# Expert sums kept in two arrays of half the columns, each block's add done as two adds

## The reference

```python
top_i, top_w = route(h2, p["w_router"], p["router_bias"])      # 8 of 64 experts per token
ffn = (routed_experts(h2, top_i, top_w, w_exp_gate, w_exp_up, w_exp_down)
       + swiglu(h2, w_sh_gate, w_sh_up, w_sh_down))              # one shared expert
x = x + g2 * ffn
# routed_experts: rows sorted by expert, each expert's rows in blocks of 128
out = lax.map(block, (row_tok, blk_exp))                         # swiglu of a block with its expert's weights
out = out.reshape(n_rows, D) * row_w[:, None]
return jax.ops.segment_sum(out, row_tok, num_segments=T + 1)[:T] # sum over a token's 8 rows
```

## Time and profile before

| | |
|---|---|
| median of three runs | 2139.46 us |
| the profiled execution | 2142.09 us, its span 2140.1 us |
| PE busy | 1930.8 us, 90% of the span |
| DVE, ACT, POOL busy | 1044.5, 871.8, 407.8 us |
| granted TensorE clock, mean | 0.955; 1.00 in every stretch of the expert stage up to 2050 us |
| expert stage | some 1104 to 2088 us of the span |
| one issue on SP, median | 0.32 us for `acc_d<-ysh`, 0.46 us for `aa<-acc_d` (9 each) |

### The profile page before, as it was taken

How to read it: one execution, slowest core, us unless ns; L and a number is a source line. 1 busy time by engine, 2 the same in 40 slices (tenths; PEclk the granted TensorE clock), 3 DMA queues, 4 the chain that set the end, 5 groups by cost and what they waited for, 6 DMA issues and landing times. The chain is left out here.

```text
span 2140.1 us, 33737 instructions
## 1 busy us (share of the span) xinstructions
PE 1930.8 (90%) x10175; PEld 1508.7 (70%) x10177; DVE 1044.5 (49%) x1519; ACT 871.8 (41%) x1181; POOL 407.8 (19%) x337
## 2 busy tenths in 40 slices
PE   3799999899899997988789999999899999999960
PEld 3799999899788565865447777666566776776740
DVE  3312401255337333555426666565555666666646
ACT  4210111333203212221246666666565666666642
POOL 0100000211111000000112333232333323223320
PEclk9899999999899998999889999999999999999985
DMA  6211221111253665325069999999999899879946
GB/s 239 71 49 49 97 70 30 34 56 50 80 190 119 222 220 197 118 100 199 0 239 386 294 298 296 368 311 374 374 330 352 281 286 287 265 236 307 283 91 257
DMA packets 154835, 433.66 MB, mean 203 GB/s; under 512 B 11551, under 2 KB 76307, under 8 KB 130210
## 3 DMA queue, kind: packets, MB, share of 16 engines
q1 hardware_dynamic: 120338, 307.40, 38.2%
q0 software_dynamic: 31776, 116.05, 21.0%
q10 hardware_dynamic: 2672, 9.57, 1.1%
HBM read 351.27 MB, written 81.72 MB: 202 GB/s over the span
## 5 line engine op out<-in xcount | busy, mean ns | idle before, releaser
L1999 DVE TENSOR_TENSOR wexp_lo<-wexp,wexp_hi 128x2048 fp32r<-128x2048 f32 x190 | 427.1, 2289 | 50.2 <-ACT wexp_hi L1951 46.7
L1951 ACT ACTIVATE wexp_hi<-wexp 128x2048 fp32r x190 | 353.0, 1905 | 55.5 <-issue 54.3
L1932 PE MATMUL bank<-wexp_down,hTe 128*128 x736 | 331.0, 592 | 1.9 <-ACT hTe L1969 1.9
L1907 PE MATMUL bank<-wexp_hi,x_hi 128*128 128x512 f32 x744 | 300.0, 403 | 3.8 <-DVE wexp_lo L1999 3.8
L1907 PE MATMUL bank<-wexp_hi,x_lo 128*128 128x512 f32 x744 | 291.6, 392 | 0.0
L1907 PE MATMUL bank<-wexp_lo,x_hi 128*128 128x512 f32 x744 | 290.1, 390 | 0.0
L1881 POOL DMA_INDIRECT acc_d<-ob,ixs x92 | 154.0, 1673 | 607.3 <-DMA acc_d<-ob,ixs 339.4
L1932 PEld LDWEIGHTS bank<-wexp_down,hTe 128*128 128x128 f32 x736 | 138.9, 189 | 142.5 <-issue 135.6
L491 PE MATMUL bank<-hT_hi,w_hi 128*128 128x344 f32 x576 | 187.2, 325 | 3.0 <-DVE w_lo L575 3.0
L491 PE MATMUL bank<-hT_hi,w_lo 128*128 128x344 f32 x576 | 185.1, 321 | 0.0
L491 PE MATMUL bank<-hT_lo,w_hi 128*128 128x344 f32 x576 | 184.5, 320 | 0.0
(11 more groups left out here) (327 smaller groups left out, 2919.3 us busy)
## 6 DMA issues: line engine op xcount, KB each, us to landing
wexp<-in_w_exp_gate SPq DMA_DIRECT2D x64, 1024.0 KB, 9.2
wexp<-in_w_exp_up SPq DMA_DIRECT2D x64, 1024.0 KB, 12.6
wexp_down<-in_w_exp_down SPq DMA_DIRECT2D x64, 1024.0 KB
wada<-in_w_ada SPq DMA_DIRECT2D x12, 2048.0 KB, 11.2
w_raw<-in_w_in SPq DMA_DIRECT2D x44, 512.0 KB, 3.9
gates_d<-gst POOLq DMA_DIRECT2D x48, 172.0 KB, 2.1
gate<-gates_d SPq DMA_DIRECT2D x16, 516.0 KB, 5.4
xn<-in_x_prompt ACTq DMA_DIRECT2D x8, 512.0 KB
```

Of the source, the lines that this page charges most:

```text
L1907: last = pe.matmul(banks[0][:].rearrange("p (g n) -> p g n", g=2), stat[:, b, k, :], mov[:, b, :, k * FF:(k + 1) * FF], start=(k == 0 and ...
L1932: last = pe.matmul(banks[4 + half][:], hT[:, f, :], wdn[:, bass.ds(slot, 1), f, half * 512:half * 512 + 512].rearrange("p a n -> p (a n)") ...
L1951: act.activation(w_hi[:, b, g, :], wexp[:, bass.ds(e & (RING - 1), 1), g, :].rearrange("p a n -> p (a n)"), ACT.Copy).then_inc(whi_ok, 1)
L1999: dve.tensor_tensor(w_lo[:, b, g, :], wexp[:, bass.ds(e & (RING - 1), 1), g, :].rearrange("p a n -> p (a n)"), w_hi[:, b, g, :], ALU.subtr ...
```

## The change

`acc_d` becomes two arrays of 1161 x 512, one for each half of the columns. Each store, load and zeroing of `acc_d` becomes one per half. POOL issues two adds per block, the first half and the second, each on its own chain: it waits for that half of `ob` and for the earlier adds of that half. The row numbers get four columns `ixs` instead of two. A new semaphore `landed` (it starts at 3) is raised by POOL when it has passed the waits of the second half; DVE waits for it with `i + 1` (POOL has come to the second half of block i - 3), ACT with `i + 3` (of block i - 1, so block i - 2 has landed).

```diff
-        acc_d = nc.dram_tensor("acc_d", [ROWS, D], F32).ap()
+        acc_d = [nc.dram_tensor(f"acc{half}_d", [ROWS, D // 2], F32).ap() for half in range(2)]
...
-                    sp.dma_start(acc_d[ROW0 + t * P:ROW0 + t * P + r, :], ysh[0:r, t % 2, :]).then_inc(stored[t % 2], 16)
+                    for c in range(2):
+                        sp.dma_start(acc_d[c][ROW0 + t * P:ROW0 + t * P + r, :],
+                                     ysh[0:r, t % 2, c * (D // 2):(c + 1) * (D // 2)]).then_inc(stored[t % 2], 16)
...
-        ixs = [tile(f"ixs{b}", [P, 1], U32) for b in range(2)]
+        ixs = [tile(f"ixs{q}", [P, 1], U32) for q in range(RING)]
...
                 tidy(pool)
+                pool.sem_inc(landed, RING - 1)
...
                     gather(i + AHEAD, (q + AHEAD) % RING)
-                    pool.wait_ge(ob_ok, 2 * i + 4)
                     pool.wait_ge(ixs_ok, i + 1)
-                    pool.wait_ge(added, 16 * i + 32)
-                    pool.sem_inc(passed, 1)
-                    pool.indirect_dma_start(out=acc_d, out_offset=bass.IndirectOffsetOnAxis(ap=ixs[b][:, 0:1], axis=0),
-                                            in_=ob[:, b, :], in_offset=None, compute_op=ALU.add).then_inc(added, 16)
+                    for half in range(2):
+                        at = slice(half * (D // 2), (half + 1) * (D // 2))
+                        pool.wait_ge(ob_ok, 2 * i + 3 + half)
+                        pool.wait_ge(added[half], 16 * i + 16)
+                        pool.sem_inc((passed, landed)[half], 1)
+                        pool.indirect_dma_start(out=acc_d[half],
+                                                out_offset=bass.IndirectOffsetOnAxis(ap=ixs[q][:, 0:1], axis=0),
+                                                in_=ob[:, b, at], in_offset=None, compute_op=ALU.add).then_inc(added[half], 16)
...
-                    act.wait_ge(ixs_ok, i + 1)
+                    act.wait_ge(landed, i + 3)
...
-                    dve.wait_ge(added, 16 * i + 16)
+                    dve.wait_ge(landed, i + 1)
                     dve.sem_inc(passed, 1)
-                    to_add(i, b)
+                    to_add(i, q)
...
-                    sp.dma_start(aa[0:r, t, :], acc_d[ROW0 + t * P:ROW0 + t * P + r, :]).then_inc(a_in[t], 16)
+                    for c in range(2):
+                        sp.dma_start(aa[0:r, t, c * (D // 2):(c + 1) * (D // 2)],
+                                     acc_d[c][ROW0 + t * P:ROW0 + t * P + r, :]).then_inc(a_in[t], 16)
```

More of the change, by code:

```diff
@@ L1454, in _ @@
                     sp.dma_start(xe_d[0:ROW0, c * (XW // 2):(c + 1) * (XW // 2)], zero[0:ROW0, :]).then_inc(stored[2], 16)
-                    sp.dma_start(acc_d[0:ROW0, c * (D // 2):(c + 1) * (D // 2)], zero[0:ROW0, 0:D // 2]).then_inc(stored[2], 16)
+                    sp.dma_start(acc_d[c][0:ROW0, :], zero[0:ROW0, 0:D // 2]).then_inc(stored[2], 16)
                     sp.dma_start(xe_d[ROW0 + TT:, c * (XW // 2):(c + 1) * (XW // 2)], zero[:]).then_inc(stored[2], 16)
@@ L1463, in _ @@
                     sp.wait_ge(y_ok, 2 * t + 2)
-                    sp.dma_start(acc_d[ROW0 + t * P:ROW0 + t * P + r, :], ysh[0:r, t % 2, :]).then_inc(stored[t % 2], 16)
+                    for c in range(2):
+                        sp.dma_start(acc_d[c][ROW0 + t * P:ROW0 + t * P + r, :],
+                                     ysh[0:r, t % 2, c * (D // 2):(c + 1) * (D // 2)]).then_inc(stored[t % 2], 16)
                 sp.wait_ge(stored[2], 16 * (TILES + 6))
                 for b in range(2):
-                    sp.wait_ge(stored[b], 16 * ((TILES + 1 - b) // 2))
+                    sp.wait_ge(stored[b], 32 * ((TILES + 1 - b) // 2))
             @block.gpsimd
@@ L1625, in _ @@
                     if t >= 2:
-                        act.wait_ge(stored[t % 2], 16 * (t // 2))
+                        act.wait_ge(stored[t % 2], 32 * (t // 2))
                     for half in range(2):
@@ L1773, in experts @@
         none = tile("none", [P, D // 4])
-        ixs = [tile(f"ixs{b}", [P, 1], U32) for b in range(2)]
-        names = "ix ixs tp xhi xlo wc whi wlo gu sg h hp hT dn ob scat wu wd pad".split()
-        (ix_ok, ixs_ok, x_tp, xhi_ok, xlo_ok, wc_ok, whi_ok, wlo_ok, gu_ps, sg_ok, h_ok, h_tp, hT_ok, dn_ps, ob_ok, added,
+        ixs = [tile(f"ixs{q}", [P, 1], U32) for q in range(RING)]
+        names = "ix ixs tp xhi xlo wc whi wlo gu sg h hp hT dn ob ld wu wd pad".split()
+        (ix_ok, ixs_ok, x_tp, xhi_ok, xlo_ok, wc_ok, whi_ok, wlo_ok, gu_ps, sg_ok, h_ok, h_tp, hT_ok, dn_ps, ob_ok, landed,
          up_ok, _, pad_ok) = (sem("s6" + n) for n in names)
+        added = [sem(f"s6add{half}") for half in range(2)]
         passed = sem("s6passed")
@@ L1855, in _ @@
                 for c in range(2):
-                    pool.dma_start(acc_d[ROW0 + TT:, c * (D // 2):(c + 1) * (D // 2)].rearrange("t (j n) -> t j n", j=2),
-                                   none[:].unsqueeze(1).to_broadcast([P, 2, D // 4])).then_inc(added, 16)
+                    pool.dma_start(acc_d[c][ROW0 + TT:, :].rearrange("t (j n) -> t j n", j=2),
+                                   none[:].unsqueeze(1).to_broadcast([P, 2, D // 4])).then_inc(added[c], 16)
                 tidy(pool)
+                pool.sem_inc(landed, RING - 1)
                 def gather(j, q):
@@ L1876, in block_of @@
                     gather(i + AHEAD, (q + AHEAD) % RING)
-                    pool.wait_ge(ob_ok, 2 * i + 4)
                     pool.wait_ge(ixs_ok, i + 1)
-                    pool.wait_ge(added, 16 * i + 32)
-                    pool.sem_inc(passed, 1)
-                    pool.indirect_dma_start(out=acc_d, out_offset=bass.IndirectOffsetOnAxis(ap=ixs[b][:, 0:1], axis=0),
-                                            in_=ob[:, b, :], in_offset=None, compute_op=ALU.add).then_inc(added, 16)
+                    for half in range(2):
[6 more added lines that the diff above has]
+                                                in_=ob[:, b, at], in_offset=None, compute_op=ALU.add).then_inc(added[half], 16)
                 blocks(pool, block_of)
                 n = pool.value_load(total[0:1, 0:1], min_val=E, max_val=ITEMS)
-                pool.wait_ge(added, 16 * n + 32)
+                for half in range(2):
+                    pool.wait_ge(added[half], 16 * n + 16)
                 for q in range(RING):
@@ L2008, in to_gather, with to_add @@
                     dve.tensor_copy(ix[q][:], lists[:, bass.ds(j, 1)]).then_inc(ix_ok, 1)
-                def to_add(j, b):
-                    dve.tensor_copy(ixs[b][:], lists[:, bass.ds(j, 1)]).then_inc(ixs_ok, 1)
+                def to_add(j, q):
+                    dve.tensor_copy(ixs[q][:], lists[:, bass.ds(j, 1)]).then_inc(ixs_ok, 1)
                 e = entry(dve, 0, 1, E - 1)
@@ L2038, in block_of @@
                     rest_of_weights(e, i + 3, 1 - b)
-                dve.wait_ge(added, 32)
                 blocks(dve, block_of)
@@ L2104, in total @@
                     acc = aa[0:r, t, :]
-                    dve.wait_ge(a_in[t], 16)
+                    dve.wait_ge(a_in[t], 32)
                     dve.tensor_tensor(acc, acc, (g2 if t < TILES - 1 else g2s)[0:r, :], ALU.mult).then_inc(prod_ok, 1)
```

## The result

Changed kernel 2148.55 us (median of 5 runs, 2144.94 to 2150.14); kernel before, on the same chip, 2138.16 (5 runs, 2135.93 to 2139.61). Ratio 1.0046, 95% interval 1.0034 to 1.0059. The forecast was 2131. The profiled execution of the changed kernel has a span of 2146.1 us, that of before 2140.1.

A forecast was written before the change was run, and what follows sets the result against it. PE was taken to lose 26.4 us in the expert stage to late-landing adds. Terms -8 + 0.3 + 1.6 - 2.1 = -8.2 us took 2142.09 to 2133.9; the median, 2.6 lower, gave 2131, range 2117 to 2149.

The forecast's parts named there:

- step 4: Expert stage: adds fall behind PE by 38x - 32.6; PE loses 16.0 us, 10.4 less than before; booked -8.
- step 3: Two blocks sharing one weight load: POOL sets the second's pace, 6.4 us; the pair takes 17.75, before 19.8.
- Step 1: How late an add may be: DVE no longer held, ACT alone is; net 0.65 us of room, once.
- Step 2: Block with its own 3 MB weight load: 24 queue turns, half packet 0.17 us; 11.35 us, before 11.04.
- Rival 1: Slower, queue turns decide: a block with its own load takes 11.9 us, PE loses 37, time 2150; chance 0.22.
- Steps 5 to 7: Shared expert's store +0.3 us; end of expert stage +1.6; last stage -2.1, as `fg` lands sooner.
- Rival 2: No change, DMA engines full: expert-stage loss stays at 26 us, time 2139; chance 0.26.
- Rival 3: Expert-stage loss goes wholly, both halves landing in under 9.4 us: -26, time 2113; chance 0.10.

The follow-up runs named there:

- the signals alone: Kernel before (whole adds) with only the changed kernel's new signals: 2144.67 us; with a one-input maximum replacing DVE's subtraction as well, 2131.30 us.
- the one-input maximum: DVE's two-input subtraction replaced in the loop by a maximum over one input: changed kernel 2132.57 us, kernel before 2136.23 us.

## Why the prediction was wrong

**The step that failed is step 4, by a term of step 3.** Step 3 priced POOL's issues in a pair at 1.58 us, and step 4 booked "3.5 for a slow issue", once, as the one of 3.55 us in the earlier trace rows had cost before. That row was the warning, and so was the gather of 1.98 beside it: both had met a subtraction. I took the slow issue for an accident and carried it over as one; it comes with nearly every issue that starts during a subtraction (72 of 78), and the old wait had kept the two apart. 35 first halves were held up, 38.8 us in sum, and PE lost 38.1 us where step 4 had 16.0 and booked 18.4. With the hold-ups taken away the changed kernel ran at 2132.6. That this is near my 2131 is in part luck: PE still lost 25.3, so the expert stage gained 1 us on the profile before and not the 8 booked. The ends of the stages made up for much of it (below), and 2 us came ahead of the expert stage, where nothing was changed. On the same chip that kernel is 4.5 us under the kernel before, where my sum had 8.2.

**Step 1, more room.** DVE waits no more, as said, but the room was no gain as long as issues were held up; without hold-ups the signals alone are 5 us faster than the old ones (2131.30 and 2136.23). ACT's later release, which I let eat a part of it, was not the matter: released at the landing itself the kernel lost as much.

**Step 2, the single.** Right: 11.35 predicted; 1514.57 to 1526.01 is 11.44. The half packet took 0.176 us for my 0.17. In 1503:1549, four singles, the queues moved

```profile
q1 hardware_dynamic: 1744, 12.71, 67.5%
q0 software_dynamic: 1743, 4.36, 36.8%
```

one packet for one packet: 1743 on 16 engines in four blocks are 27 each, the 24 and one small one at the end of each of three DMAs. So q0 got its 24 turns per block and no more. A held-up issue hides in here, as q0 is busy with the DMA before: nine singles in a row (blocks 30 to 38) are 11.43 us each, and 11.39 with the one-input maximum. Most of the 38.8 us thus cost nothing. Rival 1's price for the single (11.9) was wrong, its sum (PE loses 37, 2150 us) all but exact for another reason.

**Step 3, the pair.** The second block's first half does come soon, but the next one doesn't. First the changed kernel, then the one with the one-input maximum, at the same blocks (17 to 19): the two first halves of a pair, the second half of its second block, and the first half after it:

```profile
1315.39 1.93 POOL L1887 DMA_INDIRECT acc_d<-ob,ixs  x1 [3.15 <-DMA acc_d<-ob,ixs]
...
1321.29 1.58 POOL L1887 DMA_INDIRECT acc_d<-ob,ixs  x1 [0.48 <-issue]
1329.79 1.56 POOL L1887 DMA_INDIRECT acc_d<-ob,ixs  x1 [6.92 <-issue]
...
1336.54 3.52 POOL L1887 DMA_INDIRECT acc_d<-ob,ixs  x1 [3.89 <-DMA acc_d<-ob,ixs]
```

```profile
1310.38 1.58 POOL L1888 DMA_INDIRECT acc_d<-ob,ixs  x1 [9.49 <-DMA acc_d<-ob,ixs]
...
1315.86 1.58 POOL L1888 DMA_INDIRECT acc_d<-ob,ixs  x1 [0.72 <-DMA acc_d<-ob,ixs]
1318.54 1.56 POOL L1888 DMA_INDIRECT acc_d<-ob,ixs  x1 [1.10 <-issue]
...
1329.64 1.58 POOL L1888 DMA_INDIRECT acc_d<-ob,ixs  x1 [8.24 <-DMA acc_d<-ob,ixs]
```

5.9 us for my 6.4, then 15.25 for a single of 11.35: 21.15 us, not 17.75. Here q0 runs dry (no packet of it starts from 1320.15 to 1322.36), a late issue is not covered, and the second half hangs on the one before it. Without hold-ups this pair is 19.3 us (5.48 and 13.78). Of the four pairs at blocks 17, 24, 28 and 40, the changed kernel takes 21.2 to 22.8 us for each, the one without hold-ups 18.3 to 20.5. So 17.75 lies under the best of them, a second, smaller error.

**Step 4, the sum.** PE loses 38.1 for 16.0. 25.3 is left without hold-ups: the 12.8 between are theirs, by one execution of each, and of the 9.3 that stay I can show only the pairs as a cause, not their part. Of the 38.1, 5.7 come before block 22, where the kernel without hold-ups loses 0.1.

**Steps 5 to 7.** The store's issues took 28.18 us for 27.84: +0.3, right. The end of the stage was forecast at +1.6 and came at -1.1: from the last transposes to SP's first load of the sum 29.6 us for 30.7, although two issues of 2.92 and 1.56 us stand there. POOL went on passing the table's empty entries while they ran, so they cost no time of it. The last stage: -2.2 for -2.1 by `fg`.

**Rivals.** Rival 2's ground, engines without time to spare, holds for what is left with 4 KB packets: of 11.2 and 16.0 us of loss, 8.9 and 12.7 are waits for weights. Rival 3 was nowhere near.

## What to carry to other kernels

Before a wait is taken out, ask what it kept apart: here it held VectorE still while GpSimd issued its DMA, and with it went the alignment. One slow instance among many fast ones in a timeline is to be explained, by what ran on the other engines at that moment, before it is carried into a sum. And where a software queue's DMAs land late beside a stream of loads, the packets of the loads are the first thing to make smaller: half rows for whole ones gave 0.7%, more than any edit of the chain.

## What the hardware showed that I had not expected

- An indirect DMA's issue on GpSimd that starts while VectorE subtracts with two inputs in SBUF ends some 1.45 us after the subtraction's end (70 of the 72 long ones in the changed kernel; one stood through the next subtraction too), and it is 1.55 to 1.60 us otherwise. A maximum over one input of the same length holds up none of 87, a subtraction with one of its inputs in PSUM none of 43.
- Four pieces of 128x512 in a row can hold it up as one: 3.08 us, to the end of the last piece.
- Weights in packets of 4 KB instead of 8 KB brought an add's median landing from 10.3 to 9.1 us, and PE then waited 8.9 us for weights and for nothing else in its down matmuls.
- Where loads of several experts raise one semaphore, the profile can name a load that nobody waited for: 20.0 us in the changed kernel, where PE waited for ScalarE.
